# Six of the seven column groups of a layer's input projection as three pairs, in seven block products per pair of token tiles

## What is computed

```python
h = rmsnorm(x, p['norm1_w']) * (1 + sc1) + sh1
mq, mk, mv, mo, mi, mf, sq, sk, sv = split_proj(h @ p['w_in'])
...
q_b = rmsnorm(sq.reshape(B, T, SB_HEADS, SB_DIM), p['sb_q_norm_w'])
k_rows = rmsnorm(sk.reshape(B, T, SB_HEADS, SB_DIM), p['sb_k_norm_w'])
```

## Time and profile before

| | us |
|---|---|
| median of 3 runs | 3000.38 (2999.57 to 3002.46) |
| the profiled execution | 3003.76 |
| its span | 3002.1 |
| TensorE busy (matmul) in the span | 2890.5 (96%) |
| VectorE, ACT, GpSimd busy | 1949.0, 1267.6, 561.5 |

### The profile page before, as it was taken

How to read it: one execution, slowest core, us unless ns; L and a number is a source line. 1 busy time by engine, 2 the same in 40 slices (tenths; PEclk the granted TensorE clock), 3 DMA queues, 4 the chain that set the end, 5 groups by cost and what they waited for, 6 DMA issues and landing times.

```text
span 3002.1 us, 48951 instructions
## 1 busy us (share of the span) xinstructions
PE 2890.5 (96%) x17179; PEld 2509.2 (84%) x17179; DVE 1949.0 (65%) x3087; ACT 1267.6 (42%) x2540; POOL 561.5 (19%) x585
## 2 busy tenths in 40 slices
PE   7999999999999999999998999999999898999998
PEld 5878888887777888798887999999999897777776
DVE  2300016732998999796668777777877777777765
ACT  4611112223777888554555333333432234333332
POOL 3310003312666776320110000000000000000000
PEclk9999999999999999999999999999999999999999
DMA  6322214543522232596564444444667777555565
GB/s 219 113 79 74 73 67 154 158 138 103 148 58 59 59 80 60 193 348 197 189 213 160 152 152 152 151 151 151 207 214 247 251 241 243 180 197 182 185 211 167
DMA packets 348223, 478.51 MB, mean 159 GB/s; under 512 B 69298, under 2 KB 222072, under 8 KB 345366
## 3 DMA queue, kind: packets, MB, share of 16 engines
q1 hardware_dynamic: 331240, 423.82, 44.6%
q0 software_dynamic: 15488, 52.52, 5.2%
q10 hardware_dynamic: 1332, 0.06, 0.0%
HBM read 297.49 MB, written 178.82 MB: 159 GB/s over the span
## 4 chain that ended last, share of the span: by engine, by line
PE 45%; DVE 6%; DMA 5%; issue 1%; ACT 1%; SPq 1%; DVEq 0%; ACTq 0%
PE facc L2928 24%; PE facc L3058 6%; PE eacc L2907 6%; PE dacc L3058 4%; DMA y_out<-dres 1%; PE mpT L3081 1%; DMA fsums<-sums_d 1%; PE mpm L3090 1%; DVE fV L2439 1%; PE mpS L3100 1%; PE eyT L2890 1%; PE mpT L3131 0%; PE mpN L3116 0%; PE exT L2920 0%; DVE fV L2435 0%
## 5 line engine op out<-in xcount | busy, mean ns | idle before, releaser
L2928 PE MATMUL facc<-fright,fsums 128*128 128x416 f32 x2112 | 420.7, 355 | 18.8 <-DMA fsums<-sums_d 9.4
L767 PE MATMUL pacc<-pring,h1H 128*128 128x512 f32 x1360 | 431.0, 394 | 3.8 <-ACT h1H L326 3.8
L2928 PEld LDWEIGHTS facc<-fright,fsums 128*128 128x128 f32 x2112 | 400.3, 191 | 25.9 <-issue 19.5
L1123 DVE TENSOR_TENSOR_SCAN aC<-aB,aC,a 128x512 f32<-128x512 f32 (+3 forms) x326 | 362.8, 1113 | 12.1 <-ACT aB L1079 1.1
L1183 POOL TENSOR_TENSOR aS<-aS,aC 128x512 f32<-128x512 f32 (+3 forms) x326 | 334.5, 1034 | 152.6 <-DVE aC L1123 146.0
L767 PEld LDWEIGHTS pacc<-pring,h1H 128*128 128x128 f32 x1360 | 256.2, 189 | 56.5 <-ACT h1H L326 3.9
L2928 PE MATMUL facc<-fright,fwH 128*128 128x416 f32 x1056 | 290.1, 356 | 12.0 <-DVE fU L2423 9.6
L767 PE MATMUL pacc<-pring,h1L 128*128 128x512 f32 x640 | 248.1, 389 | 0.0
L2928 PEld LDWEIGHTS facc<-fright,fwH 128*128 128x128 f32 x1056 | 199.4, 190 | 18.0 <-issue 12.1
L1203 PE MATMUL a_z<-ak,aq 128*128 128x512 f32 (+2 forms) x616 | 199.4, 405 | 0.5 <-DMA ak<-qk_T 0.5
L368 ACT ACTIVATE pstage<-pacc 128x512 f32<-128x512 f32 x112 | 66.5, 594 | 308.1 <-PE pacc L767 308.0
(11 more groups left out here) (388 smaller groups left out, 5627.9 us busy)
## 6 DMA issues: line engine op xcount, KB each, us to landing
sums_d<-fsums SPq DMA_DIRECT2D x88, 512.0 KB, 2.9
fsums<-sums_d SPq DMA_DIRECT2D x88, 512.0 KB, 4.6
fraw<-w_up SPq DMA_DIRECT2D x66, 512.0 KB, 4.0
proj_out<-pstage SPq DMA_DIRECT2D x119, 256.0 KB, 2.0
dres<-x_d SPq DMA_DIRECT2D x92, 256.0 KB, 3.4
qk_T<-pturn POOLq DMA_DIRECT2D x68, 256.0 KB, 3.1
mwa<-w_ada SPq DMA_DIRECT2D x16, 1024.0 KB, 6.3
dpart<-act_d SPq DMA_DIRECT2D x32, 512.0 KB, 3.8
```

The source lines that it names most:

```text
L767: op = mm_(acc[:, n % NB], h[:, kk, tok(t)], weight(q, w), start=(j == 0), stop=(j == len(order) - 1))
L1123: v.tensor_tensor_scan(buf[:, a:b][:, ::-1], part(B, RB, n)[:, ::-1], nought[:, 0:width(n)], buf[:, b:b + 1], ALU.mult, ALU.add).then_inc( ...
L2928: mm = nc.tensor.matmul(bank, a[:, kk], b[:, kk], start=(begins and kk == 0 and m == 0), stop=(kk == count - 1 and m == 2), skip_group_che ...
```

## The change

Group 0 stays as it is in its products. The other six become three pairs: (1, 4), (5, 3), (6, 2). For a pair, two token tiles and one half of the inner dimension each form a block: A11 to A22 on the left (128 tokens x 512, that is 4 blocks of 128), B11 to B22 on the right (512 x 512, column of blocks = group). Seven products of sums give the four outputs:

- P1 = A11 B11, P2 = A12 B21, P3 = S4 B22, P4 = A22 T4, P5 = S1 T1, P6 = S2 T2, P7 = S3 T3
- S1 = A21 + A22, S2 = S1 - A11, S3 = A11 - A21, S4 = A12 - S2
- T1 = B12 - B11, T2 = B22 - T1, T3 = B22 - B12, T4 = B21 - T2

One such set is a *unit* (`unit`), 7 x 12 matmuls of 128 x 512; there are 8 per pair, 24 in all. The sums T of the first pair are made by VectorE during group 0 (`t_sum`), those of the other two pairs by GpSimd in units 0 to 7, in eight *events* of 4 sums (`event_sum`): SyncE loads four pieces of 256 KB, GpSimd subtracts, SyncE stores 1 MB to DRAM. The left blocks are not kept: ACT stores each plain h tile to DRAM, SyncE loads the two tiles of a coming unit, VectorE makes S1 to S4, ACT rounds seven left blocks (`left_high_of`) and VectorE makes seven low parts (`left_low_of`). ACT copies bank A to B and B to C between products (`seed_b`, `seed_c`). The sample's rows of the six groups get plain fp32 products of their own, one per event (`sample_product`, 12 events). When a pair gives way to the next, seven right blocks of 1 MB are loaded, rounded and get low parts (`cell_high_of`, `cell_low_of`), each after the product that used it.

The gates come in pieces, after tiles 3, 7, 11 and 15.

The core of the diff ("..." marks what is left out):

```diff
+    PAIRS = ((1, 4), (5, 3), (6, 2))
+    HALF = NPT // 2
+    UNITS = HALF * len(PAIRS)
+    NK = KD // 2
...
+    PRODUCTS = ("P1", "P5", "P4", "P6", "P2", "P7", "P3")
+    SIDES = {"P1": ("A11", "B11"), "P5": ("S1", "T1"), "P4": ("A22", "T4"), "P6": ("S2", "T2"), "P2": ("A12", "B21"),
+             "P7": ("S3", "T3"), "P3": ("S4", "B22")}
...
+    LEFT_HIGHS = ("A11", "S1", "A22", "S2", "A12", "S3", "S4")
+    LEFT_LOWS = ("A11", "A22", "S1", "A12", "S3", "S2", "S4")
...
+            def load_first_rows(kp):
+                sp.wait_ge(*((cell_sum, 4 * kp) if kp else (w_low, KD)))
+                for name, at in first_rows.items():
+                    sp.dma_start(at, rows_of(0, name)[:, kp]).then_inc(first_rows_in, 16)
...
+            def load_event(v):
+                if v == 0:
+                    sp.wait_ge(left_sum, 4)
+                    sp.wait_ge(left_low, 7)
+                elif v <= SUMMED:
+                    sp.wait_ge(event_stored, 16 * v)
                 else:
-                    sp.wait_ge(taken, n + 1)
-                sp.dma_start(d["proj_out"][ORDER[g], tok(t), :], stage[:, n % NS]).then_inc(stored[n % NS], 16)
+                    sp.wait_ge(sample_done, v)
+                pair, kp = EVENTS[v]
+                for a in range(2):
+                    for b in range(2):
+                        sp.dma_start(w_rows[:, a, b], d["w_in7"][PAIRS[pair][b], (2 * kp + a) * P:(2 * kp + a + 1) * P, :]
+                                     ).then_inc(event_in, 16)
+
+            def store_event(v):
+                pair, kp = EVENTS[v]
+                sp.wait_ge(cell_sum, 4 * NK + 4 * v + 4)
+                sp.dma_start(d["w1_sums"][pair - 1, kp], w_rows[:].rearrange("p a b n -> p (a b) n")).then_inc(event_stored, 16)
...
             load_x(NX - 1)
-            for q in range(KD, KD + NR):
-                load_w(q)
             for t in range(NT):
                 if t + NX < NT:
                     load_x(t + NX)
+                if t == 14:
+                    sp.wait_ge(x_turned, NT)
+                    for e in range(2):
+                        load_part(0, e)
+                if t == last:
+                    sp.wait_ge(summed, NT)
+                    load_cell(0, "B22")
+                    for e in (1, 0):
+                        load_part(1, e)
                 store(t)
-                if t == last - 2:
-                    for q in range(KD + NR, NW):
-                        load_w(q)
-            for q in range(NW, 2 * KD):
-                load_w(q)
...
+                if t % 4 == 0 and t > 0:
+                    store_gates(t // 4 - 1)
+                if t in (0, 5, 7, 9):
+                    load_first_rows((0, 5, 7, 9).index(t))
+                if t == 12:
+                    load_cell(0, "B11")
+                    load_cell(0, "B21")
+            store_gates(GATES - 1)
...
-                copy(hH[:, :, tok(t)], h_raw(t)).then_inc(h_high, 1)
...
+                if t < NPT:
+                    at_least(act, h_low, t - 1)
+                    act.dma_start(d["h1_d"][t], h_raw(t)).then_inc(h_stored[t % 2], 16)
+                copy(hH[:, t], h_raw(t)).then_inc(h_high, 1)
...
-                if t == last - 1:
-                    for q in range(KD, NW):
-                        split(q)
-                take(t)
                 if t + 2 < NT:
                     shift(t + 2)
+                if t == last - 1:
+                    left_high_of("A11", 0)
+                if t == last:
+                    for name in ("S1", "A22", "S2", "A12", "S3"):
+                        left_high_of(name, 0)
+                take(t)
                 if t + 4 < NT:
                     spread(t + 4)
...
+                if t in (5, 7, 9, 11):
+                    t_high((5, 7, 9, 11).index(t))
+                if t == 13:
+                    cell_high_of(0, "B11")
+                if t == 14:
+                    cell_high_of(0, "B21")
+            left_high_of("S4", 0)
+            cell_high_of(0, "B22")
...
+                seed_b(w)
+                if more:
+                    left_high_of("A11", n)
+                if arriving:
+                    cell_high_of(w // HALF, "T3")
+                if more:
+                    left_high_of("S1", n)
+                take_e(w)
+                if arriving:
+                    cell_high_of(w // HALF, "B22")
+                if w > FIRST:
+                    take_turned(norm_tile(w - 1, 0))
+                if w in (4, 8, 12):
+                    take_sample(w // 4 - 1)
+                if more:
+                    left_high_of("A22", n)
+                take_f(w)
...
+            def left_sum_of(n, w):
...
+                if n == 1:
+                    for e in range(2):
+                        dve.wait_ge(part_in[e], 16 * w + 16)
+                    op = v.tensor_tensor(s1, at["A21"], at["A22"], ALU.add)
+                elif n == 2:
+                    dve.wait_ge(left_sum, 4 * w + 1)
+                    op = v.tensor_tensor(s2, s1, at["A11"], ALU.subtract)
+                elif n == 3:
+                    op = v.tensor_tensor(s3, at["A11"], at["A21"], ALU.subtract)
+                else:
+                    dve.wait_ge(left_sum, 4 * w + 2)
+                    op = v.tensor_tensor(s4, at["A12"], s2, ALU.subtract)
+                op.then_inc(left_sum, 1)
...
+            def left_low_of(name, w):
...
+                top, low, own = left(name)
+                v.tensor_tensor(low, own if name[0] == "S" else h_blocks(w)[name], top.bitcast(F32), ALU.subtract).then_inc(left_low, 1)
...
+            def event_sum(name, w):
+                x_, y_ = {"T1": ("B12", "B11"), "T3": ("B22", "B12"), "T2": ("B22", "B11"), "T4": ("B21", "B22")}[name]
+                at = event_block({"T1": "B11", "T3": "B12", "T2": "B22", "T4": "B21"}[name])
+                done = 4 * NK + 4 * w
+                if name == "T1":
+                    pool.wait_ge(event_in, 64 * w + 64)
+                    pool.wait_ge(sample_done, w + 1)
+                elif name == "T2":
+                    pool.wait_ge(cell_sum, done + 2)
+                elif name == "T4":
+                    pool.wait_ge(cell_sum, done + 3)
...
+            def sample_product(v):
+
...
+                for a in range(2):
+                    for e in range(4):
+                        b, half = divmod(e, 2)
+                        op = mm_(bank_s[e * DEC:(e + 1) * DEC, 0:2 * P], h_plain[1][:, NPT, 2 * kp + a, 0:DEC],
+                                 w_rows[:, a, b, 2 * P * half:2 * P * (half + 1)], start=(kp == 0 and a == 0),
+                                 stop=(kp == NK - 1 and a == 1), skip_group_check=True)
+                op.then_inc(sample_done, 1)
...
+            def unit(w):
+                banks = {"P1": bank_a, "P5": bank_e, "P4": bank_f, "P6": bank_b, "P2": bank_a, "P7": bank_b, "P3": bank_c}
+                v = w // HALF
+                for name in PRODUCTS:
+                    one, other = SIDES[name]
...
+                    for i in range(NK):
+                        for m, (a, b) in enumerate(((0, 0), (0, 1), (1, 0))):
+                            op = mm_(banks[name], lefts[one][:, a, i], cell(other, b)[:, i],
+                                     start=(name in ("P1", "P5", "P4") and i == 0 and m == 0),
+                                     stop=(i == NK - 1 and m == 2), skip_group_check=True)
+                    op.then_inc(multiplied, 1)
+                    if name == "P5" and w > FIRST:
+                        turn(norm_tile(w - 1, 0))
+                    if name == "P4":
+                        if w in (2, 3, 5):
+                            {2: turn_ends, 3: turn_before, 5: turn_weights}[w]()
+                        if 0 < w < len(EVENTS):
+                            sample_product(w)
+                    if name == "P6" and w > FIRST:
+                        turn(norm_tile(w - 1, 1))
+                    if name == "P2" and w == 0:
+                        sample_product(0)
 
...
-            for t in range(NT):
-                project(t)
+            project(0)
+            turn_x(2)
+            for t in range(1, NT):
                 if t + 2 < NT:
                     turn_x(t + 2)
-            gates()
...
+                project(t)
+                if t % 4 == 3:
+                    gates(t // 4)
+            gates(GATES - 1)
+            for w in range(UNITS):
+                unit(w)
+            for m in range(NORMS - 2, NORMS):
+                turn(m)
```

862 lines of the change are left out of this document (601 added, 261 removed).

## The result

| | before | changed |
|---|---|---|
| median of the runs, us | 3001.42 (4 runs, 2999.57 to 3002.74) | 3085.24 (4 runs, 3082.68 to 3086.33) |
| profiled execution, us (its span) | 3003.8 (3002.1) | 3084.8 (3083.1) |
| attention's first matmul, us | 728.4 | 817.6 |
| from there to the span's end, us | 2273.7 | 2265.5 |

The changed kernel is slower by 84 us: ratio 1.0278, 95% interval 1.0261 to 1.0296. I had forecast 32 us more and a range up to 3060. The direction was right, the time lies outside. The whole difference is ahead of attention, 89 us there.

The account below looks back on a forecast made before the run. The front lasts as long as TensorE's matmuls; after the change ACT's chain bounds group 0. Terms -69 + 53 + 36 + 12 = +32 us on the median give 3032 us, range 2992 to 3060.

Parts of the forecast that it names:

- Matmuls of the six groups: Groups turned into units: 2,016 matmuls instead of 2,400, at 0.230 us each, with sample products and turns: 69 us less.
- Group 0: First group: ACT's chain from taking to taking becomes the bound, 9.3 us a turn; units start at 215.3, 53 us later.
- Rival 1: Group 0: ACT's chain does not bind, costing at most 4 us instead of 53; 2983 us in all; chance 0.13.
- Changes of pair: Units 7 to 8 and 15 to 16: renewing seven right blocks delays TensorE 10 us and 19 us.
- the clock: Around the changes of pair: 5 us added for a lowered clock after waits of 4 to 10 us.
- Rival 2: Units 8 and 16: changes of pair mostly hidden, 36 us becomes 8; 3004 us in all; chance 0.12.
- GpSimd's sums hidden: Units 0 to 7: an event takes 14 of 20 us beside the products, so it adds nothing.
- rival 4: Units 1 to 7: events over 20 us make TensorE wait for sample products, 5 us a unit; 3067 us; chance 0.03.
- VectorE does not bind: Units: VectorE has 16.4 us of work in a unit of 20.3, so it adds nothing.
- rival 3: Units 8 to 23: VectorE binds, 2.5 us too much a unit, 40 us more; 3072 us; chance 0.10.
- Tail: Last unit to attention: k's norms are no longer hidden, 16.5 us in all, 12 more; bounds 8 and 16.

Follow-up runs that it names:

- all moves together: Changed kernel plus earlier x load, sample sums at unit head, h part before w rows, second turn behind P2, blocks renewed earlier: 3005.7 us, 1.0012 times the kernel before.
- the kernel with two low buffers: Changed kernel with five reordering edits and a second buffer for turned tiles' low parts, the study's fastest: 2985.4 us, 0.9955 times the kernel before.
- the last experiment: Against the kernel with five moves and second low buffer: sample products behind P6, last four a unit later: 2986.1 us, 0.9950 times the kernel before.

## Why the prediction was right, and where it was wrong

- **Matmuls of the six groups** (-69): right in kind, 7 us too small. I took 0.230 us a matmul between 0.2267 and 0.2333. All seven products run at 2.72 us for 12, the lower bound. The turns, 0.48, were right; the sample products, 1.1, measured 1.26.
- **Group 0** (+53, measured +64): the step holds. Takings were foretold 9.3 us apart and are 9.2; unit 0 at 215 came at 227. Rival 1, that this chain does not bind, is out. Mis-sized were the turns with new loads: I priced first rows, blocks and their rounding at 23 us, measured is 31, because SyncE does not only transfer ahead of x, it also *waits* there, 4.3 and 2.1 us, until VectorE has made the sums of the rows before (the last one runs from 131.12 to 131.81). One of these sums took 2.88 us, where the next took 0.69, while GpSimd made a low part (128.00 to 130.54), as in seven other kernels with this group 0. The first taking came 2 later and the end took 2 more. SyncE's queue, then VectorE and GpSimd:

```profile
127.20 0.34 SPq L365 DMA_DIRECT2D proj_out<-pstage  x1
131.84 0.81 SPq L376 DMA_DIRECT2D praw<-w_in  x2
132.69 0.91 SPq L376 DMA_DIRECT2D pturn<-w_in  x2
133.65 0.43 SPq L356 DMA_DIRECT2D px<-x_all  x1
```

```profile
128.20 2.88 DVE L856 TENSOR_TENSOR pT_plain<-pturn,pT_plain 128x512 f32<-128x512 f32 x1
128.00 2.54 POOL L1102 TENSOR_TENSOR h1L<-h_plain,h1H 128x1024 fp32r<-128x1024 f32 x1 [6.58 <-DMA h_d<-h_plain]
131.12 0.69 DVE L858 TENSOR_TENSOR pT_plain<-pturn,pT_plain 128x512 f32<-128x512 f32 x1
```

- **Changes of pair** (29 + 5 for the clock; 39 by leaving them out): the step holds, 19 for unit 16 was 23.7 with the clock. It was too small in unit 8, where the renewal costs 15.4 instead of 10. Rival 2, mostly hidden, is out. The bound from bandwidth I had left out altogether: with four blocks in the queue, a T block took 10.4 us to land (median of the four in units 7 and 8) though the DMA moved 378 to 416 GB/s from 397 to 411 us.
- **GpSimd's sums hidden** (0): this step failed. I compared the event's 14 us with a unit's 20, and did not follow what stands *behind* it in SyncE's queue: the h part. Its late arrival held ACT, and ACT held bank C and the sample's squares. Loading the part first gave 10.5 us of the 19 in units 1, 4 and 5 back. The 5 us of unit 1 are another wait: for the w rows themselves, 3.1 us and a slow product after it; they went without the sums (20.6) and with the sample product later (21.7), not with the part first. That is rival 4's mechanism, in one unit instead of seven; its price of 35 us did not come.
- **The squares of the sample's sums**: not in my sum. They cost 9 us in unit 8. In unit 4 the wait and the slow products after it are nearly 8 us in the trace, but moving them alone gave 1.6 in units 0 to 7; with the h part first and all moves together unit 4 fell from 24.2 to 20.3, so about 4 are theirs. I had listed the sample product only by TensorE's 1.1 us, not by the wait ahead of it.
- **VectorE does not bind** (0; rival 3: 40 us): between the two. In the plain units it has the time, as the last stage of the kernel with two low buffers shows (TensorE 139.81 of 140 us). But units 9 to 15 and 17 to 23 still lost 16 us by one single buffer and a turn placed one product too early. I had named that buffer, in the tail only. At the change to unit 16 it has none to spare in the best kernel, 23.52 of 24 us, much as my chain for that unit had it.
- **Tail** (+12): 12.4, right.

So the sum failed by terms that it had at nothing, the hand-overs of the h part and the w rows, the squares and the low buffer, and by the sizes of group 0 and of the changes of pair. The direction came out right by mechanisms that it did name: group 0 and the changes of pair alone outweigh the matmuls.

Ahead of attention the forecast was 57 us short. Hand-overs that it did not list make about 9 for the squares in unit 8, 19 in units 1, 4 and 5 (about 10 for the h part, 5 for the w rows, 4 for the squares), 16 for the low buffer and the early turn; sizes make 11 in group 0 and 5 in the changes of pair, less 7 for the matmuls; 4 are small terms. Each hand-over is told apart by a kernel above; the 11 and the 7 are read from the trace alone. In the best kernel unit 0 still starts 20.5 us later than group 1 did before (183.1 against 162.6), unit 1 takes 6 us too much, units 8 and 16 take 11 and 17, and the tail 9.5. For unit 16 VectorE's unbroken work is the likely cause; no kernel here leaves a part of it out. The rest is open. In unit 8 the last experiment shows only that it is not the w rows alone; other ways to renew the blocks were not tried.
